# Gates of a hybrid decoder layer with tokens in rows and two of them in seven block products, with the first loads in quarter pieces

## The reference

```python
proj = einsum('bsd,dc->bsc', x, w_in)     # cb, cc, ch, hq, hf, hi, hg, mq, ga, gb, gc
y_a = short_conv(...); y_b = hgrn2(...)
y_c = memory_attention(mq, mem @ w_mem_k, mem @ w_mem_v)
merged = (sigmoid(ga + b_ga) * (y_a @ w_branch[0])
          + sigmoid(gb + b_gb) * (y_b @ w_branch[1])
          + sigmoid(gc + b_gc) * (y_c @ w_branch[2]))
x = layer_norm(ALPHA * x + merged @ w_o, ln1_g, ln1_b)
h = square(relu(x @ w_up))
x = layer_norm(ALPHA * x + h @ w_down, ln2_g, ln2_b)
```

## Time and profile before

| | |
|---|---|
| median of 3 runs | 843.17 us (842.96 to 843.2) |
| profiled execution | 844.07 us, of it 842.3 us span from first to last instruction |
| PE, DVE, ACT, POOL busy | 98%, 60%, 41%, 2% of the span |
| mean granted PE clock | 0.996 of full |

### The profile page before, as it was taken

One profiled execution on the slowest core, in us unless ns is written; L12 is line 12 of the kernel. 1 busy time (PEld: TensorE's weight loads), 2 busy tenths in 40 slices (PEclk: granted clock), 3 DMA queues, 4 the chain that ended last, 5 costly groups with the idle time before them and its releaser, 6 DMA issues.

```text
span 842.3 us, 10120 instructions
## 1 busy us (share of the span) xinstructions
PE 823.8 (98%) x4089; PEld 698.4 (83%) x4089; DVE 502.7 (60%) x553; ACT 348.5 (41%) x390; POOL 19.8 (2%) x30
## 2 busy tenths in 40 slices
PE   6999999999999999999999999999999999999994
PEld 6989888889888888888888889888888888888883
DVE  3637636567255424424337675986578666956698
ACT  3639334475136223222225024652545354435530
POOL 1100100000001000000000000000000000000000
PEclk9999999999999999999999999999999999999998
DMA  9541312322122332233631506017301820280002
GB/s 321 180 150 51 100 36 68 115 68 71 43 100 67 133 101 100 100 100 100 245 135 72 197 1 218 32 43 258 100 1 51 279 71 1 62 288 0 1 1 100
DMA packets 67095, 87.52 MB, mean 104 GB/s; under 512 B 1485, under 2 KB 50678, under 8 KB 67062
## 3 DMA queue, kind: packets, MB, share of 16 engines
q1 hardware_dynamic: 67062, 87.06, 30.6%
HBM read 84.96 MB, written 2.10 MB: 103 GB/s over the span
## 4 chain that ended last, share of the span: by engine, by line
PE 94%; DVE 4%; issue 1%; DMA 0%; ACT 0%; DVEq 0%
PE bank L1248 30%; PE bank L1250 30%; PE bank L1249 30%; PE bank L1395 1%; DVE two L1148 1%; DVE two L1160 1%; DMA two<-in_mem_dram 0%; DVE w_lo L747 0%; PE bank L1440 0%; PE bank L1391 0%; PE bank L1508 0%; PE bank L1361 0%; PE bank L1277 0%; DVE two L1165 0%; DVE decay L1154 0%
## 5 line engine op out<-in xcount | busy, mean ns | idle before, releaser
L1248 PE MATMUL bank<-x_hi,w_hi 128*128 128x512 f32 (+1 forms) x704 | 269.5, 383 | 0.0
L1250 PE MATMUL bank<-x_hi,w_lo 128*128 128x512 f32 (+1 forms) x704 | 267.4, 380 | 0.0
L1249 PE MATMUL bank<-x_lo,w_hi 128*128 128x512 f32 (+1 forms) x704 | 267.4, 380 | 0.0
L742 DVE TENSOR_TENSOR w_lo<-raw,w_hi 128x2048 fp32r<-128x2048 f32 x43 | 98.3, 2291 | 115.0 <-ACT w_hi L464 114.7
L1250 PEld LDWEIGHTS bank<-x_hi,w_lo 128*128 128x128 f32 x704 | 132.4, 188 | 25.1
L1249 PEld LDWEIGHTS bank<-x_lo,w_hi 128*128 128x128 f32 x704 | 132.6, 188 | 24.0
L1248 PEld LDWEIGHTS bank<-x_hi,w_hi 128*128 128x128 f32 x704 | 132.6, 188 | 24.0
L1248 PE MATMUL bank<-w_hi,y_hi 128*128 128x512 f32 (+1 forms) x320 | 121.6, 380 | 0.4 <-DVE two L1148 0.4
L1250 PE MATMUL bank<-w_hi,y_lo 128*128 128x512 f32 (+1 forms) x320 | 121.2, 379 | 0.0
L1249 PE MATMUL bank<-w_lo,y_hi 128*128 128x512 f32 (+1 forms) x320 | 121.1, 379 | 0.0
L464 ACT ACTIVATE w_hi<-raw 128x2048 fp32r<-128x2048 f32 x43 | 82.2, 1916 | 52.5 <-PE bank L1250 36.8
(11 more groups left out here) (178 smaller groups left out, 835.9 us busy)
## 6 DMA issues: line engine op xcount, KB each, us to landing
raw<-in_w_in_dram SPq DMA_DIRECT2D x28, 1024.0 KB, 5.0
raw<-in_w_up_dram SPq DMA_DIRECT2D x16, 1024.0 KB, 7.8
small<-in_w_down_dram SPq DMA_DIRECT2D x12, 1024.0 KB, 7.1
raw<-in_w_branch_dram SPq DMA_DIRECT2D x6, 1024.0 KB, 4.9
two<-in_x_dram SPq DMA_DIRECT2D x2, 2048.0 KB, 12.3
raw<-in_w_o_dram SPq DMA_DIRECT2D x4, 1024.0 KB, 5.0
raw<-in_w_down_dram SPq DMA_DIRECT2D x4, 1024.0 KB, 4.6
raw<-in_w_mem_v_dram SPq DMA_DIRECT2D x2, 1024.0 KB, 7.7
```

Source lines behind the costliest of these rows:

```text
L742: dve.tensor_tensor(w_lo[:, slot, :], raw[:, r, :], w_hi[:, slot, :].bitcast(F32), ALU.subtract)\
L1248: pe.matmul(dst, a[0], b[0], start=first, stop=False, skip_group_check=goes_on)
L1249: pe.matmul(dst, a[0], b[1], start=False, stop=False, skip_group_check=goes_on)
L1250: return pe.matmul(dst, a[1], b[0], start=False, stop=last, skip_group_check=goes_on)
```

## The change

- Gates: tokens are now in the rows of every gate and branch tile (x is the operand that stands in the array, a block of w of 4 x 128 rows and 512 columns moves). The bias is a row, copied to all partitions (`gate_bias`), and is added by DVE as it reads the tile into `acc`; the sigmoid is taken in place. The loop over gates is written out.
- Gate 0 has the 8 tiles of 24 matmuls. Gates 1 and 2 take seven products (m1 to m7) of 2 x 12 matmuls, in banks 4 to 7 (m2 in 0 and 1), on sums of weight blocks made by DVE (`gate_sum`) and four combinations of x blocks made by DVE once, in gate 0 (`x_difference`, `x_further`), which lie in free places of `w_hi`, `x_hi` and `y_hi`. DVE adds the products up from the banks (`seven_read`).
- Slabs of gates use three slots in turn; the loads wait for places named one by one.
- `merged` has tokens in rows and is transposed by PE per block of tokens (`merged_transposed`), 8 transpositions each, then split from the banks (`merged_parts`).
- `resid` shares its place with `acc`, so x is loaded again per block once that block is merged.
- Start: mem, w_mem_k in quarters in turn, second slab in two halves, x and w_mem_v in halves in turn; PE makes transpositions of the identity (`keep_busy`) among them.

```diff
+FIRST = ("k1n1", "k2n1", "k1n2", "k2n2")
+SEVEN = ("m1", "m2", "m5", "m6", "m3", "m7", "m4")
+FIRST_SLOT = (0, 1, 2, 3, 0, 2)
+NEXT_SLOT = (3, 0, 2, 3, 0, 2, 3, 0, 2)
+OUT_SLOT = (3, 1, 0, 2)
+SEVEN_BANK = dict(m1=4, m6=4, m7=4, m4=4, m5=6, m3=6, m2=0)
...
 @block.sync
+            for j in range(4):
+                part = slice(j * 256, (j + 1) * 256)
+                sp.dma_start(mem_tok[:, :, part], mem[0].rearrange("(b p) d -> p b d", p=P)[:, :, part])\
+                    .then_inc(mem_landed[j], 16)
+                part = slice(2 * j, 2 * j + 2)
+                sp.dma_start(raw[:, 0, :].rearrange("p (k c) -> p k c", k=KD)[:, part], wmk[:, part, 0:256])\
+                    .then_inc(front_landed[j], 16)
...
+            def out_load(n):
+                e, h = n // 2, n % 2
+                sp.wait_ge(slab_lo, (gate_slab(2, "br%d" % (n + 1)) if n < 2 else S_OUT + n - 2) + 1)
+                raw_load(h, wout[:, 4 * h:4 * h + 4, e * WID:(e + 1) * WID], 4)
+
+            out_load(0)
+            out_load(1)
+            sp.wait_ge(gate_read, seven_tile(2, "m4", 1) + 1)
+            sp.wait_ge(slab_lo, gate_slab(2, "m4") + 1)
             for n, v in enumerate((ln1_g, ln1_b, ln2_g, ln2_b)):
                 sp.dma_start(ln_par[:, n, :], v.to_broadcast((P, D))).then_inc(ln_landed, 16)
-            for e in range(2):
-                for h in range(2):
-                    load(S_OUT + 2 * e + h, h, wout[:, 4 * h:4 * h + 4, e * WID:(e + 1) * WID], 4)
+            for b in range(TB):
+                sp.wait_ge(merge_done, 8 + 2 * (b + 1))
+                sp.dma_start(resid[:, b, :], x_t[:, b, :]).then_inc(x_again[b], 16)
+            out_load(2)
+            out_load(3)
...
 @block.scalar
+            out_hi(0)
+            out_hi(1)
+            merged_parts(0)
             merged_parts(1)
-            hi(S_OUT + 3, 2, OUT_ROUND * MAIN)
+            act.wait_ge(gate_done, branch_tile(2, 3, 1) + 1)
+            out_hi(2)
+            merged_parts(2)
+            out_hi(3)
+            merged_parts(3)
...
 @block.vector
+            for b in range(TB):
+                for e in range(2):
+                    branch(2, b, e)
+                if b < 2:
+                    out_lo(b)
+                if b:
+                    merged_parts(b - 1)
+            out_lo(2)
+            out_lo(3)
+            merged_parts(TB - 1)
...
 @block.tensor
+            def keep_busy(n):
+
+                for _ in range(n):
+                    pe.transpose(bank[3][:, 0:P], ident[:], ident[:])
+
+            pe.wait_ge(ident_ready, 1)
+            keep_busy(10)
+            mem_transposed(0)
+            for j in range(4):
+                if j < 3:
+                    mem_transposed(j + 1)
+                if j < 2:
+                    keep_busy(8 - 4 * j)
+                aux_copied(pe, PRO, "t%d" % j)
+                if j < 3:
+                    pe.wait_ge(front_lo, j + 1)
+                else:
+                    slab(0)
...
+            def seven(i):
+                for name in SEVEN:
+                    slab(gate_slab(i, name))
+                    if i == 1 and name in XFORMS:
+                        pe.wait_ge(form_split, XFORMS.index(name) + 1)
+                    for r in range(2):
+                        n = seven_tile(i, name, r)
+                        dst = gate_bank(n)
...
+                        opens = name in ("m1", "m5", "m2")
+                        for k in range(4):
+                            mm = three(dst, x_part(name, k, r), w_part(gate_slot(i, name), k * WID, WID),
+                                       opens and k == 0, k == 3, not opens)
+                        mm.then_inc(gate_done, 1)
+
+            def merged_transposed(b):
+                pe.wait_ge(merge_done, 8 + 2 * (b + 1))
+                for j in range(2):
+                    t = begin_aux(MGT, "g%d%d" % (b, j))
+                    for k in range(4):
+                        c = (4 * j + k) * P
+                        tr = pe.transpose(t[:, k * P:(k + 1) * P], merged[:, b, c:c + P], ident[:])
+                    tr.then_inc(aux_done, 1)
+
+            branch_of(0)
+            seven(1)
+            branch_of(1)
+            seven(2)
+            slab(gate_slab(2, "br2"))
+            pe.wait_ge(gate_read, seven_tile(2, "m4", 1) + 1)
+            for b in range(TB):
+                for e in range(2):
+                    branch_part(2, b, e)
+                if b > 1:
+                    merged_transposed(b - 2)
```

More of the change, by code:

```diff
@@ L617, in merged_parts, with gate_hi @@
-            def merged_parts(h):
-                for k in range(4 * h, 4 * h + 4):
-                    act.wait_ge(merge_done, 1 + 2 * KD + k + 1)
-                    act.activation(y_hi[:, k, :], merged[:, k, :], ACT.Copy).then_inc(merged_hi, 1)
-            with act.Fori(0, 2) as i:
-                gates(i, False)
-            gates(2, True)
-            hi(S_OUT + 2, 3)
-            merged_parts(1)
-            hi(S_OUT + 3, 2, OUT_ROUND * MAIN)
+            def gate_hi(i, name, src, tiles):
+                act.wait_ge(gate_done, tiles)
+                act.activation(w_hi[:, gate_slot(i, name), :], src, ACT.Copy).then_inc(slab_hi, 1)
@@ L1002, in merged_parts, with stepped @@
[L1002 to L1013 removed]
+            form_steps = [0]
+            def stepped(ins):
+                ins.then_inc(form_stepped, 1)
+                form_steps[0] += 1
+                dve.wait_ge(form_stepped, form_steps[0])
@@ new lines, in branch @@
+            def branch(i, b, e):
+                n = branch_tile(i, b, e)
+                w = 8 * i + branch_order(i).index((b, e)) + 1
+                part = merged[:, b, e * WID:(e + 1) * WID]
+                dve.wait_ge(gated, gated_at(i, b, e))
+                t = read(n)
+                if i == 0:
+                    dve.tensor_tensor(part, acc_of(b, e), t, ALU.mult).then_inc(gate_read, 1)
+                    return
+                dve.tensor_tensor(acc_of(b, e), acc_of(b, e), t, ALU.mult).then_inc(gate_read, 1)
+                dve.wait_ge(gate_read, n + 1)
+                dve.tensor_tensor(part, part, acc_of(b, e), ALU.add).then_inc(merge_done, 1)
@@ new lines, in merged_parts, with begun @@
+            def merged_parts(b):
+                for j in range(2):
+                    dve.wait_ge(merged_hi, 2 * b + j + 1)
+                    n = "g%d%d" % (b, j)
+                    part = (slice(None), slice(4 * j, 4 * j + 4), slice(b * P, (b + 1) * P))
+                    low_of(y_lo[part], bank[MGT.bank[n]].rearrange("p (k t) -> p k t", k=4), y_hi[part])\
+                        .then_inc(aux_read[MGT.bank[n]], 1)
+            def begun(i):
+                gate_lo(i, "m1", gate_a)
+                gate_sum(i, "m5")
@@ new lines, in _, with out_lo @@
+            xform_lo_of("m3")
+            seven(1)
+            branch(1, 0, 0)
+            begun(2)
+            for b in range(1, TB):
+                branch(1, b, 0)
+            gate_lo(2, "m2", raw[:, 1, :])
+            for b in range(TB):
+                branch(1, b, 1)
+            seven(2)
+            def out_lo(n):
+                dve.wait_ge(slab_hi, S_OUT + n + 1)
+                slot = OUT_SLOT[n % 4]
+                low_of(w_lo[:, slot, :], raw[:, n % 2, :], w_hi[:, slot, :]).then_inc(slab_lo, 1)
@@ new lines, in gate_bank, with branch_part @@
+            def gate_bank(n):
+                if gate_before(n):
+                    pe.wait_ge(gate_read, gate_before(n))
+                return bank[GATE_BANK[n]]
+            def branch_part(i, b, e):
+                n = branch_tile(i, b, e)
+                dst = gate_bank(n)
+                for k in range(HEADS):
+                    mm = three(dst, both(y_hi, y_lo, ALL, i * HEADS + k, block_of(b)),
+                               w_part(gate_slot(i, "br%d" % (e + 1)), k * WID, WID), k == 0, k == HEADS - 1)
+                mm.then_inc(gate_done, 1)
@@ new lines, in _ @@
+            for e in range(2):
+                for b in range(TB):
+                    n = first_tile(b, e)
+                    dst = begin(OUT_ROUND, n) if n < MAIN else gate_bank(n)
+                    for k in range(KD):
+                        name = FIRST[2 * e + k // 4]
+                        if b == 0 and k % 4 == 0:
+                            slab(gate_slab(0, name))
+                        mm = three(dst, both(x_hi, x_lo, ALL, k, block_of(b)),
+                                   w_part(gate_slot(0, name), (k % 4) * WID, WID), k == 0, k == KD - 1)
+                    mm.then_inc(gate_done, 1)
```

585 lines of the change are left out of this document (406 added, 179 removed).

## The result

| | median | executions |
|---|---|---|
| before | 843.25 us (842.94 to 843.52) | 8 |
| changed | 845.89 us (845.34 to 847.12) | 8 |

The ratio is 1.0032 (interval 1.0024 to 1.0041): 2.6 us slower.

A forecast was written before the change was run, and what follows sets the result against it. TensorE (PE), busy 98% of the span, was taken as the bound. On the profiled 844.07 us, -10.9 + 3.5 + 1.0 + 7.8 + 2.7 - 2.7 = +1.4 gave 845.5, as a median 844.6 us; range 839.0 to 850.0.

The forecast's parts named there:

- likeliest case: The forecast's own case, given a 33% chance, with its own range of 842.5 to 846.5 us.
- 48 matmuls fewer: Gates 1 and 2: seven products save 24 matmuls each, 0.2265 us apiece, -10.9 us.
- 32 transpositions: Turning the merged sum on PE: 32 transpositions of 0.109 us that nothing hides, +3.5 us.
- drain at the last m4: End of gate 2: PE waits for DVE's read of the last m4 before the last branch product, +1.0 us.
- wait for w_o slab 2: Output stage: load queued behind block 3's x reload, PE idle +7.8 us until F+40.3; F: PE's start of last branch products.
- clock after it: Output stage: after the w_o wait PE restarts at 1.2 GHz for 5.9 us, +2.7 us.
- gates: Gates: DVE's added splits, sums and reads fit beside PE's work if no slab comes late, 0 us.
- start: First loads in quarters with dummy transpositions: clock rises by about 9.5 us, slab 1 done at 22.3, -2.7 us.
- the wait is not there: Rival, output stage: w_o slab 2 is loaded in time, the queue order having been misread; 834.1 us, chance 12%.
- the wait is shorter: Rival, output stage: w_o wait of 5 to 6.5 us and the clock falls little; 841.0 us, chance 18%.
- rival of late gates: Rival, gates: three slots serve all slabs, 14 slabs each 0.4 us late, 5.6 us; 850.2 us, chance 10%.
- identity transpositions do not bring the clock up: Rival, start: dummy transpositions leave the clock at half, 1.0 instead of -2.7 us; 848.3 us, chance 22%.

The follow-up runs named there:

- 48 again: Late wait with the chains of m1 made twice in gates 1 and 2, 48 matmuls of 512 columns more: 846.07 us.
- twice: Late wait with each of the 32 transpositions of `merged` made twice: 838.67 us.
- late wait: Early w_o with PE's wait for DVE's read of the last m4 moved behind block 1's branch products, where that bank is first written: 834.62 us.
- busy in the wait: Changed kernel with 64 identity transpositions on PE where it waits for w_o slab 2, the load staying late: 843.84 us.
- early w_o: Changed kernel with the loads of w_o slabs 2 and 3 placed behind the x reloads for blocks 0 and 1 instead of all four: 836.18 us.
- bridge: Late wait with 10 identity transpositions between those of mem's first and second quarter, and 4 instead of 8 behind the second: 835.04 us.
- value first: Bridge with each half of w_mem_v loaded ahead of the half of x: 833.82 us.
- old start: Changed kernel with the earlier kernel's first loads and first products for mem and w_mem_k, no identity transpositions; x, w_mem_v still in halves: 848.04 us.

## Why the prediction came out as it did

The forecast of 844.6 us was 1.3 below the median, inside the likeliest case's range, and its direction was right. Its sum, term by term:

| term | forecast | in the profiled execution or by an experiment | by medians |
|---|---|---|---|
| 48 matmuls fewer | -10.9 | -10.9 (48 again: 10.88) | -11.45 |
| 32 transpositions | +3.5 | +3.5 (twice: 3.52) | +4.05 |
| drain at the last m4 | +1.0 | +1.1 (late wait) | +1.6 |
| wait for w_o slab 2 | +7.8 | +7.3 idle, 7.5 with drain and restart | |
| clock after it | +2.7 | +1.4; 1.5 and 3.1 in two others | about 2.7 (busy in the wait) |
| gates | 0 | 0; 0.9 and 1.0 in two other profiles | |
| start | -2.7 | +0.2 | about -1.2 |

The 7.5 is the stretch of the changed kernel less that of early w_o (468.13 - 26.44 = 441.69), 8.9, less 1.4 for the clock. In the profiled execution the terms then add up to +2.8 us, for 2.9 between the spans. That the total came so near is in part luck: in that execution the start was 2.9 us worse than forecast, and the wait and the clock 0.3 and 1.3 better.

- **The wait for w_o** held in every link, in size too: the order of SP's list, the position of block 2's pair ahead of the slab on DVE, and the restart at F+40.2. The text counts four half tiles of PE from F+24.4; its F+32.6 goes with three, and three it was (idle from 457.0, F+32.9). Early w_o removed it by moving two transfers and nothing else. The rivals "the wait is not there" and "the wait is shorter" (5 to 6.5 us) fell at once.
- **The clock** was right in kind. Of three profiles with this wait two showed half of the forecast's size (1.4 and 1.5) and one a little more than it (3.1). Early w_o and late wait together take 11.27 us off the medians: 1.1 for the drain and 7.5 for the wait leave 2.7, as busy in the wait has it. The medians carry the differing starts too, so that the term was about right over many executions is likely and not shown.
- **The gates** took DVE's 66 us of new work without a wait on PE in the changed kernel. That the place is as tight as the slack of "in a bank 0.3 us" said was seen in two other profiles: a load 1 us late there left PE idle for 0.55 and 0.64 us and cost 0.9 and 1.0 with drain and restart. The rival of late gates is this in small, far from its 5.6 us.
- **The start** is the step that was mis-sized. By medians it was forecast 1.5 us too good, which is the whole miss of the total: "If the clock rises by about 9.5, because PE has then worked since 1.8". PE had not worked since 1.8: it paused 2.4 us for the second quarter of mem, which took 5.4 us from issue to landing where bytes at 349 GB/s had given 5.7 us after the start of the span. The clock rose at 13.2. The five other profiles with the same start (early w_o, busy in the wait, late wait, twice, 48 again) have the second quarter at 6.0 to 7.0 and full pace for good from 6.0 to 11.9. x's second transposition is at 26.44 to 29.84 in the six, 28.1 in the mean, for 29.63 before, so the gain lies between none and 3.2 us. That the pause held the clock down is argued: behind pauses of 0.99, 1.97 and 2.04 us the transpositions at 6.01, 6.75 and 6.83 already ran at full pace, though the last two executions (busy in the wait and 48 again) fell back to half from about 8.1 to 11.8.
- **The rival "identity transpositions do not bring the clock up"** came out split. As placed in the change they do nothing measurable (two experiments). But transpositions did bring it up: in bridge and in value first, without a pause, those at 6.93 and 6.57 already ran at the pace of full clock, before any matmul, and so did those at 6.01, 6.75 and 6.83 behind a pause. The evidence for the rival, half the pace behind mem's 16 transpositions, was one execution: old start has the same 16 and full pace behind them. The Trainium skill, "TensorE: Matmul & The Clock Gate", section "Part 4: PE-mode transpose", says that full clock does not engage for transpositions; these rows disagree, and so do the 64 that held it in the w_o wait, and the measurement decides. The same page of the Trainium skill says in its section "HAM oscillation — how this bites in real kernels" that a wait for data drops the clock and the next burst starts slow; the rows from 464.31 to 467.32 agree.

Still open: why the rise at the start, and the return after the same idle time (2.7 or 6.1 us), differ between executions of like programs. Bridge and value first have one profile each, so that a pauseless start always brings the clock up early is not shown, nor that it does so oftener than the change's own. What the start of before is worth exactly is also only argued.

## What to carry to other kernels

When a transfer in an in-order queue gets a wait on the end of a stage, list everything queued behind it: 1 MB weights behind a 0.5 MB reload turned a gain of 7.1 us into a loss of 2.6 here. A PE wait of several us costs its length and then some matmuls at half clock, so look for it first among loads that used to wait for nothing. Compare a start-up edit on a kernel without other chance waits, by the distance between two marks in the trace rather than by whole times: whole times of one kernel wandered by 0.9 to 3.4 us here, while the distance from x to the turned sum was 410.88 or 410.89 in three kernels with equal gates. Look for a small wait in it first, as two other profiles had one.

## What the hardware showed that I had not expected

- 64 transpositions of the identity kept the granted clock full through a wait of 8 us, the last 1.0 of it idle (clock 1.00 in each window, matmuls 0.23 apart behind it), and behind an unbroken row of 24 from 1.53 on it was up before the first matmul in two kernels. Behind 14 and a pause of 1.0 to 2.0 us it was up in three more, and in two of these it fell back to half within 2 us, in the middle of PE's work.
- After an idle 7.3 and 7.5 us the half clock lasted 2.7 us in two executions and 6.1, after 7.5, in a third, with the same matmuls behind it.
- The windows of the first 13 us show a granted clock of 1.00 while the matmuls stand 0.21 apart; in that stretch only the cadence tells the clock. In busy in the wait, where full pace came first, the windows from 8 to 9 and 9 to 10 us do show 0.57 and 0.50. The changed kernel:

```profile
11.00:13.00 2.00, 2.00 (x11) 2.00 (x11) 0.00 (x0) 0.00 (x0) 0.00 (x0) 1.00 1.09 371
13.00:15.00 2.00, 2.00 (x19) 2.00 (x18) 0.95 (x2) 1.12 (x2) 0.00 (x0) 1.00 1.05 378
```

11 instructions of PE in 2 us, then 19, at the same printed clock.
